# Modulation products on TensorE in four column groups of 32, with the first gate's row made per block

## The chip, the cores and the metric

The kernel runs on one core of a Trainium2 chip. Its time is device microseconds (us) of one execution of the program; before the change the median of 3 runs is 2649.36 us (2646.62 to 2649.52). The engines are TensorE (PE: matmuls; PEld is its weight load, which overlaps them), VectorE (DVE), ScalarE (ACT), GpSimd (POOL) and SyncE (SP), which here issues every DMA, in program order.

## The reference, cut to what matters

Two transformer-like blocks over x of 256 tokens by 2048 features, in fp32. The change lies in the first block, whose norms and gates are modulated by a vector c:

```python
c_act = jax.nn.silu(c)                       # 1 x 2048
mod = c_act @ w_ada[l] + b_ada[l]            # w_ada: 2048 x 12288 (96 MB)
sh1, sc1, gt1, sh2, sc2, gt2 = jnp.split(mod, N_MOD, axis=-1)
h = modulate(rmsnorm(x, g_norm_mix[l]), sh1, sc1)
proj = h @ w_in[l]                           # 2048 x 3072
...                                          # convolution, RG-LRU, gelu gate, pooling mixer
y = jnp.concatenate([y_lru, y_pool], axis=-1) @ w_out[l]
x = x + gt1[:, None, :] * y
h = modulate(rmsnorm(x, g_norm_ffn[l]), sh2, sc2)
f = (jax.nn.silu(h @ w_ffn_gate[l]) * (h @ w_ffn_up[l])) @ w_ffn_down[l]
x = x + gt2[:, None, :] * f
```

So a matrix of 96 MB is multiplied by one row. sh1 and sc1 are needed before w_in, gt1 after w_out's first block of columns, the rest for the feed-forward part.

## The kernel before, in words

The big matrices are streamed once, in tiles of 1 MB, through four slots (`raw`). ACT rounds each half tile to `w_hi` (`split_hi`, L634), DVE takes the rest into `w_lo` (`split_lo`, L1803), and PE forms three products per chunk (hi·hi, lo·hi, hi·lo). A matrix is a `Phase`: blocks of 512 columns, each of 8 halves; a half is 24 matmuls of 256 columns in w_in (`features_half`, L1175 to L1177) and 12 of 512 columns in the others (`tokens`, L1200 to L1202). `stream`, `mixer` and `beside` functions hang other work between the halves; the order is written out by hand, there is no scheduler.

The modulation matrix comes in tiles of 128 x 1024 (512 KB). A unit `a` is 1024 of its output columns, 16 tiles deep; there are 12 units, 192 tiles.

- **First stage** (units 0 to 3 in the order `MOD_ORDER`, 64 tiles, eight slots: `mod_raw` and `mod_more`): nothing else can start before shift and scale are known. 26 of the tiles go to PE (`first_product`, L1305): the stationary operand is a column of `c_silu` spread over 128 columns, so all 128 rows of the result are equal. The other 38 go to DVE (L2043, L2047), which multiplies a tile by a scalar per partition and adds it to `mod_acc`. DVE adds PE's row to it (`add_rows`, L2060), and PE sums `mod_acc` over the partitions with `ones` as the moving operand (`first_sums`, L1313). Between the products stand x's transposes (`TURN0_AT`) and w_in's first halves (`W_IN_AT`); the fourth half follows the last sums.
- **Later** (units 4 to 11, 128 tiles, the four `mod_raw` slots): all on DVE, beside the halves (`mod_product`, L2017 and L2021). `mod_places` says how many tiles each half carries: 48 beside w_in's 48 halves, 48 beside w_out's 32, 32 in the feed-forward part. PE sums a unit when it is done (`mod_sums`, L1293), DVE adds the bias (`mod_result`).
- **The first gate**: after w_in PE spreads all 16 chunks of gt1 over the partitions (`rows_of`, L1273), ACT copies them to `row` (L884) before it splits w_out's next halves, and DVE uses `row` after each block of w_out (`add_gated`, L2230, L2232).

SP issues a modulation tile once the tile four (first stage: eight) before it has been used, and a weight tile once DVE has taken `w_lo` of the one in its slot (L516). The queue is in order: a tile whose slot isn't free holds back whatever is behind it.

Of the kernel before, what the change touches and what calls it, by code (L numbers as in the profile page):

```python
# [26 lines left out]
P = 128  # L27
# [5 lines left out]
LEAD = 3  # L33
# [53 lines left out]
def two_blocks(nc, d, out):  # L87
# [58 lines left out]
    mod_places = [2, 1, 1, 1, 2, 1, 1, 1] * 3 + [1, 1, 1, 0, 1, 1, 1, 0] * 3 + [2] * 20 + [1] * 8 + [0] * 4 + [1, 0] * (4 * up1.halves)  # L146
    assert MOD_FIRST * KC + sum(mod_places) == MOD_BLOCKS * KC and MOD_FIRST == 4 and MOD_BLOCKS == 12

    MOD_ORDER = [0, 2, 1, 3]
    FIRST_SLOTS = 2 * MOD_SLOTS  # L150
    mod_on_pe = [k in ((1, 3, 5, 7, 9, 11, 13, 15), (1, 4, 7, 10, 13))[i // 2] for i in range(MOD_FIRST) for k in range(KC)]
    FIRST_BY_DVE = mod_on_pe.count(False) + MOD_FIRST
    ROWS_AFTER = 14

    def mods_used(s):

        own = mod_on_pe[:s + 1].count(mod_on_pe[s])
        return own if mod_on_pe[s] else own + (s // KC + (s % KC > ROWS_AFTER))

    def mods_of_pe(i, k=KC):  # L160
        return mod_on_pe[i * KC:i * KC + k].count(True)

    def steps_of_dve(i):

        return mod_on_pe[:i * KC].count(False) + i

    def mod_at(place):

        n = MOD_FIRST * KC + sum(mod_places[:place])
        return range(n, n + mod_places[place])  # L170

    with ExitStack() as ctx:
# [21 lines left out]
        row = at("row", R, [P, D])  # L194
# [24 lines left out]
        gt2 = at("gt2", F + 90, [P, COLS])  # L219
# [25 lines left out]
        res_tmp = at("res_tmp", F + 88, [P, T, COLS])  # L245
# [60 lines left out]
        def first_rows(i):  # L306
            return (pair[:, 0], pair[:, 1], misc[:, 2:4], pair[:, 1])[i]
# [27 lines left out]
        def columns(tile, widths):  # L335
# [4 lines left out]
        ssq, var, std, rstd, c_silu, g_mod, ls8, nls8, window_inv, ssq_parts, scale, squared = columns(  # L340
            keep, [T, T, T, T, KC, KC, RC, RC, 16, T * 4, T, T])
# [33 lines left out]
        row_mm, row_ready, gt2_row, fin_x = (sem(n) for n in ("row_mm", "row_ready", "gt2_row", "fin_x"))  # L375
# [38 lines left out]
        GT2_AT = 1  # L414
# [34 lines left out]
        def _(pool):  # L449
# [5 lines left out]
            pool.memset(vec_rows[:], 0.0).then_inc(zeroed, 1)  # L455
            done(pool.memset(upper[:], 1.0))
# [5 lines left out]
                               pattern=[[1, P]], channel_multiplier=-1).then_inc(consts, 1)  # L462

# [17 lines left out]
        CONSTS = 6 + HALF_ROPE  # L481
# [3 lines left out]
        def _(sp):  # L485
            ada = d["w_ada"][0].rearrange("(k p) n -> p k n", p=P)

            def slot_free(s):

                sp.wait_ge(mod_used if mod_on_pe[s] else mod_step, mods_used(s))  # L490

            def load_first(s):
                if s >= FIRST_SLOTS:
                    slot_free(s - FIRST_SLOTS)
                sp.dma_start(first_slot(s), ada[:, s % KC, bass.ds(MOD_ORDER[s // KC] * MOD_COLS, MOD_COLS)]).then_inc(mod_landed[s % FIRST_SLOTS], 16)

            def load_mod(a, k):
                j = (a - MOD_FIRST) * KC + k
                if j < MOD_SLOTS:
                    slot_free(MOD_FIRST * KC - FIRST_SLOTS + j)  # L500
                else:

                    sp.wait_ge(mod_step, FIRST_BY_DVE + j + 1 - MOD_SLOTS)
                sp.dma_start(mod_raw[:, k % MOD_SLOTS, :], ada[:, k, bass.ds(a * MOD_COLS, MOD_COLS)]).then_inc(mod_landed[k % MOD_SLOTS], 16)
# [27 lines left out]
            def load_mods(place):  # L532
                if 0 <= place < len(mod_places):
                    for n in mod_at(place):
                        load_mod(n // KC, n % KC)
# [85 lines left out]
        def _(act):  # L621
# [100 lines left out]
            def norm_beside(n, gain=None):  # L722

                def finish(b, c):
                    if b:
                        norm_sums(n, b - 1)
                        norm_turned(n, b - 1, gain)
                return finish

# [61 lines left out]
            for t in range(T):  # L791
                run(xn_sq[:, t, :], x[:, t, :], ACT.Square, accum_out=ssq[:, t:t + 1]).then_inc(n_ssq, 1)
            act.wait_ge(vec_turned, 1)
# [12 lines left out]
            run(sin_t, ang_r, ACT.Sin).then_inc(prep_exp, 1)  # L806
            for b in range(XB):
                norm_turned(0, b)
            for q in range(XG):
                norm_high(0, q)  # L810
                if q < XG // 2:
                    split_hi(w_in, 0, [q])
                if q == XG // 2 - 1:
                    split_hi(w_in, 0, [4])
# [4 lines left out]
            def mixer(b):  # L819

                for n in range(w_in.halves):
# [4 lines left out]
                    beside(b, n)  # L826
                act.wait_ge(w_used, w_in.end(b))
# [55 lines left out]
            act.wait_ge(row_mm, 1)  # L883
            run(row[:], flat(misc[:]), ACT.Copy).then_inc(row_ready, 1)  # L884


            stream(w_out, norm_beside(1), up1)
# [14 lines left out]
            def beside_down1(b, place):  # L902
# [4 lines left out]
                if place == (GT2_AT if b else LAST_HIDDEN + 1):  # L907
                    act.wait_ge(gt2_row, b + 1)
                    if b:
                        act.wait_ge(res_ready, w_out.blocks + b)  # L910
                    run(gt2[:], misc[:, 2, :], ACT.Copy).then_inc(row_ready, 1)
# [249 lines left out]
        def _(pe):  # L1161
# [98 lines left out]

            def gt2_rows(b):

                pe.wait_ge(mod_ready, 10)
                if b:
                    pe.wait_ge(row_ready, b + 1)
                for m in range(4):
                    mm = pe.transpose(misc[:, 2, m * P:(m + 1) * P], mod[:, 5 * KC + 4 * b + m:5 * KC + 4 * b + m + 1].to_broadcast([P, P]), ident[:])
                mm.then_inc(gt2_row, 1)

            def rows_of(col, signal):  # L1270

                for m in range(KC):
                    mm = pe.transpose(misc[:, m // 4, (m % 4) * P:(m % 4 + 1) * P], col[:, m:m + 1].to_broadcast([P, P]), ident[:])  # L1273
                mm.then_inc(signal, 1)

# [11 lines left out]
            def mod_sums(a, c, read=None):  # L1287
                pe.wait_ge(mod_step, FIRST_BY_DVE + (a - MOD_FIRST) * KC + KC)
                if read:

                    pe.wait_ge(mod_ready, read)
                for m in range(MOD_M):
                    mm = pe.matmul(misc[:, 3, bass.ds(a * MOD_M + m, 1)], mod_acc[:, c, m * P:(m + 1) * P], ones[:, 0:1],  # L1293
                                   start=True, stop=True, skip_group_check=True)
                mm.then_inc(mod_mm, 1)

            def first_product(i, k):
# [3 lines left out]
                if i == 3 and not mods_of_pe(i, k):  # L1301

                    pe.wait_ge(mod_ready, 2)
                for e in range(2):
                    mm = pe.matmul(first_rows(i)[:, e, :], c_silu[:, k:k + 1].to_broadcast([P, P]), first_slot(s)[:, e * COLS:(e + 1) * COLS],  # L1305
                                   start=(mods_of_pe(i, k) == 0), stop=(mods_of_pe(i, k) + 1 == mods_of_pe(i)))
                mm.then_inc(mod_used, 1)

            def first_sums(i):

                pe.wait_ge(mod_step, steps_of_dve(i + 1))
                for m in range(MOD_M):
                    mm = pe.matmul(first_rows(i)[:, 0, m:m + 1], mod_acc[:, i % 2, m * P:(m + 1) * P], ones[:, 0:1],  # L1313
# [1423 lines left out]
```

## Time and profile before

| what | value |
|---|---|
| median of 3 runs | 2649.36 us |
| profiled execution, and its span | 2653.23 us, 2651.5 us |
| PE, DVE, ACT busy | 97%, 63%, 47% of the span |
| DMA | 549.44 MB, 207 GB/s over the span |
| mean granted TensorE clock | 0.987 |

The profile divides the program into a long part that PE fills and a beginning that it doesn't:

```profile
PE   6799989999999999999999999999999999999998
DVE  4788897674544455565777676546666666644444
ACT  2236335444444444444566655445555555544453
DMA  9997897886555555565534544555555555555554
```

Each digit is a fortieth of the span (66 us), in tenths busy. The first six are what the change is about: the first stage, w_in and w_out, with DMA at 0.9 and DVE high. From the seventh on, PE is full. Busy time of PE adds up matmuls that overlap in its pipeline, so idle time understates what is free there, and matmul counts over a stretch say more.

### The profile page before, as it was taken

The page shows a single profiled execution, that of the slowest core. Times are in us where ns is not written, and L with a number is a line of the kernel's source. Part 1 is how long each engine was busy: PE and PEld are TensorE (multiplying, and loading weights), DVE is VectorE, ACT ScalarE, POOL GpSimd, SP SyncE. Part 2 cuts the span into 40 slices and gives each one's busy share as a digit, 9 for nine tenths or more (in the row PEclk, how much of TensorE's full clock was granted, in tenths as well). Part 3 has the DMA queues.
Part 4 walks back from the last instruction along what each step waited for, and adds up shares of the span by engine and source line. Part 5 has one row for each costly group of instructions (what it writes and reads, how often), then busy time and mean ns, then how long its engine had stood idle before and what let it go on. Part 6 is the DMA issues. An engine that isn't in the chain of part 4 may idle for free.

```text
span 2651.5 us, 32416 instructions
## 1 busy us (share of the span) xinstructions
PE 2573.7 (97%) x12334; PEld 2127.8 (80%) x12334; DVE 1658.0 (63%) x1963; ACT 1257.5 (47%) x1637; POOL 5.6 (0%) x24
## 2 busy tenths in 40 slices
PE   6799989999999999999999999999999999999998
PEld 3589767888888888888888888888888888888877
DVE  4788897674544455565777676546666666644444
ACT  2236335444444444444566655445555555544453
POOL 0000000000000000000000000000000000000000
PEclk9899999999999999999999999999999999999999
DMA  9997897886555555565534544555555555555554
GB/s 346 359 365 262 317 365 240 283 270 198 188 187 188 189 186 187 186 206 175 164 123 128 159 127 137 185 192 186 190 186 180 188 181 183 186 186 186 187 194 143
DMA packets 350140, 549.44 MB, mean 207 GB/s; under 512 B 18496, under 2 KB 200784, under 8 KB 349264
## 3 DMA queue, kind: packets, MB, share of 16 engines
q1 hardware_dynamic: 350032, 547.94, 61.6%
q8 instruction: 75, 1.23, 0.2%
q14 instruction: 33, 0.27, 0.0%
HBM read 545.79 MB, written 2.10 MB: 207 GB/s over the span
## 4 chain that ended last, share of the span: by engine, by line
PE 84%; DVE 6%; DMA 6%; ACT 2%; issue 1%; SPq 1%; ACTq 0%; DVEq 0%
PE pair L1200 25%; PE pair L1202 25%; PE pair L1201 25%; DMA mod_raw<-in_w_ada 3%; DMA mod_more<-in_w_ada 2%; DVE mod_acc L2021 2%; DVE w_lo L1803 1%; PE pair L1730 1%; PE misc L1659 1%; PE misc L1783 1%; PE pair L1175 0%; ACT w_hi L634 0%; PE pair L1177 0%; PE pair L1176 0%; PE pair L1305 0%
## 5 line engine op out<-in xcount | busy, mean ns | idle before, releaser
L1803 DVE TENSOR_TENSOR w_lo<-raw,w_hi 128x1024 fp32r<-128x1024 f32 x848 | 1017.6, 1204 | 848.6 <-ACT w_hi L634 847.5
L634 ACT ACTIVATE w_hi<-raw 128x1024 fp32r<-128x1024 f32 x848 | 882.4, 1043 | 1091.5 <-PE pair L1202 1000.6
L1200 PE MATMUL pair<-w_hi,a_hi 128*128 128x512 f32 x2048 | 810.9, 396 | 6.7 <-DVE w_lo L1803 3.8
L1202 PE MATMUL pair<-w_hi,a_lo 128*128 128x512 f32 x2048 | 799.7, 390 | 0.0
L1201 PE MATMUL pair<-w_lo,a_hi 128*128 128x512 f32 x2048 | 798.7, 390 | 0.0
L1200 PEld LDWEIGHTS pair<-w_hi,a_hi 128*128 128x128 f32 x2048 | 385.5, 188 | 87.7 <-DVE w_lo L1803 5.0
L1202 PEld LDWEIGHTS pair<-w_hi,a_lo 128*128 128x128 f32 x2048 | 385.4, 188 | 81.7
L1201 PEld LDWEIGHTS pair<-w_lo,a_hi 128*128 128x128 f32 x2048 | 385.9, 188 | 78.0 <-issue 1.0
L1200 PE MATMUL pair<-w_hi,hid_hi 128*128 128x512 f32 x704 | 275.0, 391 | 0.0
L1202 PE MATMUL pair<-w_hi,hid_lo 128*128 128x512 f32 x704 | 274.0, 389 | 0.0
L1201 PE MATMUL pair<-w_lo,hid_hi 128*128 128x512 f32 x704 | 273.9, 389 | 0.0
L2021 DVE SCALAR_TENSOR_TENSOR mod_acc<-mod_raw,keep,mod_acc 128x1024 f32<-128x1024 f32 x120 | 153.8, 1282 | 16.8 <-DMA mod_raw<-in_w_ada 13.9
L1202 PEld LDWEIGHTS pair<-w_hi,hid_lo 128*128 128x128 f32 x704 | 132.2, 188 | 27.4
L1200 PEld LDWEIGHTS pair<-w_hi,hid_hi 128*128 128x128 f32 x704 | 132.2, 188 | 27.2
L1201 PEld LDWEIGHTS pair<-w_lo,hid_hi 128*128 128x128 f32 x704 | 132.2, 188 | 27.1
L1175 PE MATMUL pair<-a_hi,w_hi 128*128 128x256 f32 x384 | 115.1, 300 | 11.6 <-DVE w_lo L1803 11.6
L1176 PE MATMUL pair<-a_lo,w_hi 128*128 128x256 f32 x384 | 111.5, 290 | 0.0
L1177 PE MATMUL pair<-a_hi,w_lo 128*128 128x256 f32 x384 | 111.3, 290 | 0.0
L1175 PEld LDWEIGHTS pair<-a_hi,w_hi 128*128 128x128 f32 x384 | 76.9, 200 | 14.2 <-DVE w_lo L1803 13.1
L1176 PEld LDWEIGHTS pair<-a_lo,w_hi 128*128 128x128 f32 x384 | 76.8, 200 | 1.1 <-issue 1.0
L1177 PEld LDWEIGHTS pair<-a_hi,w_lo 128*128 128x128 f32 x384 | 76.6, 200 | 0.0
L1200 PE MATMUL pair<-w_hi,ya_hi 128*128 128x512 f32 x128 | 50.6, 395 | 0.9 <-DVE w_lo L1803 0.9
(369 smaller groups left out, 2148.7 us busy)
## 6 DMA issues: line engine op xcount, KB each, us to landing
raw<-in_w_in SPq DMA_DIRECT2D x88, 1024.0 KB, 5.4
raw<-in_w_up SPq DMA_DIRECT2D x176, 512.0 KB, 4.4
mod_raw<-in_w_ada SPq DMA_DIRECT2D x160, 512.0 KB, 6.8
raw<-in_w_out SPq DMA_DIRECT2D x48, 1024.0 KB, 5.1
raw<-in_w_ffn_gate SPq DMA_DIRECT2D x88, 512.0 KB, 3.6
raw<-in_w_ffn_up SPq DMA_DIRECT2D x88, 512.0 KB, 4.7
raw<-in_w_ffn_down SPq DMA_DIRECT2D x32, 1024.0 KB, 5.1
raw<-in_w_down SPq DMA_DIRECT2D x32, 1024.0 KB, 5.1
```

Source lines behind the costliest of these rows:

```text
L634: run(w_hi[:, h % HALF_SLOTS, 0:n, :], raw[:, h // 2 % RAW_SLOTS, at0:at0 + n, :], ACT.Copy).then_inc(hi_ready, 1)
L1175: pe.matmul(o, wh, hi[:, k, :], start=(h == kk == 0 and m % 2 == 0), stop=False, skip_group_check=True)
L1176: pe.matmul(o, wh, lo[:, k, :], start=False, stop=False, skip_group_check=True)
L1177: mm = pe.matmul(o, wl, hi[:, k, :], start=False, stop=(h == ph.halves - 1 and kk == n - 1), skip_group_check=True)
L1200: pe.matmul(o, hi[:, own], w_hi[:, slot, kk, :], start=(h == kk == 0), stop=False)
L1201: pe.matmul(o, hi[:, own], w_lo[:, slot, kk, :], start=False, stop=False)
L1202: mm = pe.matmul(o, lo[:, own], w_hi[:, slot, kk, :], start=False, stop=(h == ph.halves - 1 and kk == n - 1))
L1659: mm = pe.matmul(misc[:, h // 8, (h % 8) * SP:(h % 8 + 1) * SP], decay[:, h, :], xdt[:, c, h, :], start=True, stop=True, skip_group_check= ...
L1730: mm = pe.transpose(pair[:, c, m // 2, m % 2 * S + t * P:m % 2 * S + (t + 1) * P], ff_t[:, t, m * P:(m + 1) * P], ident[:])
L1783: mm = pe.matmul(misc[:, j, :], p_f[:, k, t * P:(t + 1) * P], w_ple[:, k, j * COLS:(j + 1) * COLS], start=(k == 0), stop=(k == PLE // P - 1))
L1803: dve.tensor_tensor(w_lo[:, slot, 0:n, :], raw[:, h // 2 % RAW_SLOTS, at0:at0 + n, :], w_hi[:, slot, 0:n, :].bitcast(F32), ALU.subtract).t ...
L2021: dve.scalar_tensor_tensor(out=acc, in0=of, scalar=by, in1=acc, op0=ALU.mult, op1=ALU.add).then_inc(mod_step, 1)
```

## The change

All 64 tiles of the first stage, and 32 of the later 128 (units 5 and 6), are multiplied on PE. The stationary operand is now a column of `c_silu` spread over 32 columns, and each product writes 32 partitions of one bank: an even tile's two halves of columns write partitions 0 to 31 and 32 to 63, an odd tile's the other two quarters. ACT copies the bank to `mod_rows` (`mod_out`), and four small matmuls with `mod_rows` stationary and `groups` (a 128 x 2 matrix of ones at partitions 0 and 64, and 32 and 96) moving add the quarters and turn the row into columns (`mod_turn`). Sixteen tiles that stood beside w_out now stand beside w_in. gt1's row is made for one block of 512 columns at a time.

```diff
-    mod_places = [2, 1, 1, 1, 2, 1, 1, 1] * 3 + [1, 1, 1, 0, 1, 1, 1, 0] * 3 + [2] * 20 + [1] * 8 + [0] * 4 + [1, 0] * (4 * up1.halves)
+    mod_places = [2, 1, 1] * (IN_PLACES // 3) + [2, 1, 1, 1, 1, 1, 1] * 4 + [0] * 4 + [1, 0] * (4 * up1.halves)
+    MOD_BY_PE, MOD_BY_DVE = [5, 6], [4, 7, 8, 9, 10, 11]
+        order = "PPD" * 8 + "D" * 8 + "DDPP" * 8 + "D" * 32 + "D" * 32
...
+            def mod_product(k, tile, bank):
+                for e in range(2):
+                    own = slice((2 * (k % 2) + e) * (P // 4), (2 * (k % 2) + e + 1) * (P // 4))
+                    mm = pe.matmul(bank[own], c_silu[:, k:k + 1].to_broadcast([P, P // 4]), tile[:, e * COLS:(e + 1) * COLS],
+                                   start=(k < 2), stop=(k >= KC - 2), skip_group_check=True)
+                mm.then_inc(mod_used, 1)
...
+            def mod_turn(a, count):
+                pe.wait_ge(mod_turned, count)
...
+                for m in range(MOD_M // 2):
+                    mm = pe.matmul(mod_cols(a)[:, m:MOD_M:MOD_M // 2], mod_rows[:, m * P:(m + 1) * P], groups,
+                                   start=True, stop=True, skip_group_check=True)
...
+            def mod_pair(n):
+                for j in (n - 1, n):
+                    pe.wait_ge(mod_landed[j % MOD_SLOTS], 16 * (FIRST_TILES // FIRST_SLOTS + j // MOD_SLOTS + 1))
...
+                for j in (n - 1, n):
+                    mod_product(mod_seq[j][1], mod_raw[:, j % MOD_SLOTS, :], misc[:, 3, :])
...
             for i in range(MOD_FIRST):
                 for k in range(KC):
-                    if mod_on_pe[i * KC + k]:
-                        first_product(i, k)
+                    first_product(i, k)
+                    if i and k == 1:
+                        mod_turn(MOD_ORDER[i - 1], i)
...
-                first_sums(i)
+            mod_turn(MOD_ORDER[MOD_FIRST - 1], MOD_FIRST)
             first_w_in(3)
...
+                def beside_w_in(h):
+                    if b == 0 and h == 4:
+                        pe.wait_ge(mod_ready, MOD_FIRST)
+                        mods_beside(0)
+                    mods_beside(b * w_in.halves + h - LEAD)
...
-            rows_of(mod[:, 2 * KC:3 * KC], row_mm)
...
-                    dve.tensor_tensor(res_tmp[:], pair[:, c], row[:, None, cols].to_broadcast([P, T, COLS]), ALU.mult).then_inc(res_ready, 1)
+                dve.tensor_tensor(pair[:, c], pair[:, c], gt[:, None, :].to_broadcast([P, T, COLS]), ALU.mult).then_inc(res_ready, 1)
```

Where a unit's sums and results fall is set by `SUMS_AT` and `RESULT_AT`. On DVE the first stage keeps the norm of x and loses its 38 products.

PE's queue at the program's start, before (`pair` is the PSUM result, `keep` holds `c_silu`, `mod_more_79` and `_80` are the further slots):

```order
L1305 MATMUL pair<-mod_raw,keep 128x512 x4
L1305 MATMUL pair<-mod_more_79,keep 128x512 x2
L1305 MATMUL pair<-mod_more_80,keep 128x512 x2
L1305 MATMUL pair<-mod_raw,keep 128x512 x4
L1305 MATMUL pair<-mod_more_79,keep 128x512 x2
L1284 MATMUL misc<-ident,vec_rows 128x128 x7
L1305 MATMUL pair<-mod_more_80,keep 128x512 x2
L1313 MATMUL pair<-ones,mod_acc 128x1 x8
```

and now (two rows per tile, so x8 is four tiles):

```order
L1347 MATMUL pair<-mod_raw,keep 32x512 x8
L1347 MATMUL pair<-mod_more_78,keep 32x512 x4
L1347 MATMUL pair<-mod_more_79,keep 32x512 x4
L1347 MATMUL pair<-mod_raw,keep 32x512 x8
L1347 MATMUL pair<-mod_more_78,keep 32x512 x4
L1320 MATMUL misc<-ident,vec_rows 128x128 x7
L1347 MATMUL pair<-mod_more_79,keep 32x512 x4
L1347 MATMUL pair<-mod_raw,keep 32x512 x4
L1339 MATMUL misc<-keep,mod_rows 128x2 x4
```

PE has twice the products per unit, a quarter as wide, and the sums of a unit stand behind the first two tiles of the next.

DVE's queue where w_in's first block is under way, before (`w_lo` is the half's split, `mod_acc` a modulation tile, `a_lo` the normalised x):

```order
L1899 TENSOR_TENSOR a_lo<-features_70,a_hi 128x512 x2
L2017 TENSOR_SCALAR mod_acc<-mod_raw,keep 128x1024
L2021 SCALAR_TENSOR_TENSOR mod_acc<-mod_raw,keep,mod_acc 128x1024 x3
L1803 TENSOR_TENSOR w_lo<-raw,w_hi 128x1024
L2021 SCALAR_TENSOR_TENSOR mod_acc<-mod_raw,keep,mod_acc 128x1024
L1803 TENSOR_TENSOR w_lo<-raw,w_hi 128x1024
L2021 SCALAR_TENSOR_TENSOR mod_acc<-mod_raw,keep,mod_acc 128x1024 x2
L1803 TENSOR_TENSOR w_lo<-raw,w_hi 128x1024
```

and now:

```order
L1983 TENSOR_TENSOR a_lo<-features_69,a_hi 128x512 x2
L2102 TENSOR_SCALAR mod_acc<-mod_raw,keep 128x1024
L1886 TENSOR_TENSOR w_lo<-raw,w_hi 128x1024
L2106 SCALAR_TENSOR_TENSOR mod_acc<-mod_raw,keep,mod_acc 128x1024
L1886 TENSOR_TENSOR w_lo<-raw,w_hi 128x1024 x3
L2106 SCALAR_TENSOR_TENSOR mod_acc<-mod_raw,keep,mod_acc 128x1024
L1886 TENSOR_TENSOR w_lo<-raw,w_hi 128x1024 x2
```

Two of three modulation tiles there are gone from DVE. They stand in PE's queue, two tiles (four products) at a time between w_in's halves:

```order
L1214 MATMUL pair<-a_hi,w_hi 128x256
L1215 MATMUL pair<-a_lo,w_hi 128x256
L1216 MATMUL pair<-a_hi,w_lo 128x256
L1347 MATMUL misc<-mod_raw,keep 32x512 x4
L1214 MATMUL pair<-a_hi,w_hi 128x256
L1215 MATMUL pair<-a_lo,w_hi 128x256
L1216 MATMUL pair<-a_hi,w_lo 128x256
```

Of the 16 such pairs, 15 stand in w_in and one behind w_out's third half. Of the first eight, six stand two halves behind the one before, one three halves; from the ninth on they are three apart.

## Rows read from the trace of the kernel before

**Rows 1.** Stretches: busy us of PE, PEld, DVE, ACT, POOL; PEclk, DMA share, GB/s.

```profile
0.00:60.00 60.00, 41.05 (x102) 18.92 (x103) 26.27 (x52) 16.76 (x20) 5.56 (x24) 0.91 0.91 339
60.00:116.00 56.00, 42.37 (x181) 26.64 (x180) 41.24 (x46) 9.52 (x12) 0.00 (x0) 0.87 1.03 404
116.00:187.00 71.00, 61.89 (x458) 61.28 (x459) 61.86 (x76) 27.09 (x33) 0.00 (x0) 0.88 0.93 337
187.00:285.00 98.00, 95.08 (x734) 92.22 (x734) 88.16 (x92) 56.82 (x77) 0.00 (x0) 1.00 0.81 290
285.00:404.00 119.00, 105.17 (x474) 84.38 (x473) 106.74 (x92) 43.47 (x50) 0.00 (x0) 0.96 0.93 339
430.00:700.00 270.00, 270.00 (x1232) 224.14 (x1231) 167.62 (x150) 114.55 (x121) 0.00 (x0) 1.00 0.75 250
```

**Rows 2.** The same view, shorter stretches of the first stage and one of w_in.

```profile
25.00:35.00 10.00, 5.45 (x17) 2.10 (x15) 2.37 (x3) 0.18 (x1) 0.16 (x1) 1.00 0.82 293
45.00:50.00 5.00, 5.00 (x10) 2.02 (x10) 2.57 (x2) 4.97 (x5) 0.00 (x0) 0.76 0.79 270
...
60.00:100.00 40.00, 32.14 (x132) 18.67 (x130) 32.05 (x38) 8.47 (x11) 0.00 (x0) 0.87 1.03 407
...
202.00:222.00 20.00, 20.00 (x168) 19.97 (x167) 14.05 (x13) 17.60 (x28) 0.00 (x0) 1.00 0.74 262
```

**Rows 3.** Order of time, PE: one tile's products; start, us, instruction.

```profile
97.51 1.88 PE L1305 MATMUL pair<-mod_more,keep 128*128 128x512 f32 x4
```

**Rows 4.** The chain that ended last, from 105 us: start, us, what.

```profile
96.80 11.46 DMA mod_more<-in_w_ada
...
108.29 1.29 DVE mod_acc L2047
...
109.68 1.22 DVE mod_acc L2060
...
110.99 1.30 DVE mod_acc L2047
...
112.33 3.59 PE pair L1313 x16
```

**Rows 5.** Groups of instructions, DVE, 116 to 285 us: busy, mean ns, idle before.

```profile
L2021 DVE SCALAR_TENSOR_TENSOR mod_acc<-mod_raw,keep,mod_acc 128x1024 f32<-128x1024 f32 x45 | 57.7, 1282 | 8.0 <-DMA mod_raw<-in_w_ada 7.2
L1803 DVE TENSOR_TENSOR w_lo<-raw,w_hi 128x1024 fp32r<-128x1024 f32 x46 | 56.2, 1223 | 10.7 <-ACT w_hi L634 10.7
```

**Rows 6.** Order of time, ACT: results of w_in's blocks 0, 2, 3, 5 leave PSUM.

```profile
138.75 1.93 ACT L784 ACTIVATE xc<-pair,vec 128x256 f32<-128x256 f32 x4 [2.04 <-PE pair L1177]
...
193.01 1.02 ACT L871 ACTIVATE xp<-pair 128x1024 f32<-128x1024 f32 x1 [1.98 <-PE pair L1177]
...
225.35 1.02 ACT L877 ACTIVATE xp<-pair 128x1024 f32<-128x1024 f32 x1 [1.76 <-PE pair L1177]
...
283.56 1.02 ACT L881 ACTIVATE y_lru<-pair 128x1024 f32<-128x1024 f32 x1 [2.03 <-PE pair L1177]
```

**Rows 7.** DMA issues, 122 to 290 us: count, KB each, median us to landing.

```profile
mod_raw<-in_w_ada SPq DMA_DIRECT2D x48, 512.0 KB, 6.8
raw<-in_w_in SPq DMA_DIRECT2D x18, 1024.0 KB, 7.4
```

**Rows 8.** Order of time, DVE: the longest wait for a tile in w_in.

```profile
155.76 1.28 DVE L2021 SCALAR_TENSOR_TENSOR mod_acc<-mod_raw,keep,mod_acc 128x1024 f32<-128x1024 f32 x1 [5.89 <-DMA mod_raw<-in_w_ada]
```

**Rows 9.** Groups of instructions, 122 to 290 us: small work on PE, the row copy.

```profile
L1293 PE MATMUL misc<-ones,mod_acc 128*128 128x1 f32 x32 | 3.7, 245 | 0.0
...
L1273 PE MATMUL misc<-ident,mod 128*128 128x128 f32 x16 | 2.0, 276 | 0.0
...
L884 ACT ACTIVATE row<-misc 128x2048 f32<-128x2048 f32 x1 | 1.9, 1867 | 0.0
```

**Rows 10.** Groups of instructions, 290 to 410 us: DVE's modulation products beside w_out.

```profile
L2021 DVE SCALAR_TENSOR_TENSOR mod_acc<-mod_raw,keep,mod_acc 128x1024 f32<-128x1024 f32 x45 | 57.7, 1283 | 8.0 <-DMA mod_raw<-in_w_ada 5.8
```

**Rows 11.** Chain of waits, 385 us: x's eight transposes beside a block of w_out.

```profile
385.88 1.09 PE misc L1230 x8
```

## What I expect of the change

> **What bounds the kernel now.** I read the busy time by stretches first, then the order of time at the seams, the groups of instructions, and last the landing times of the DMAs.
>
> [rows 1] cut the first 430 us at the seams of the stages. To 116 us only x's transposes, three halves of w_in and modulation products run, and DMA is the limit: 404 GB/s at a share of 1.03 from 60 us on. In the first 60 us it is 339 GB/s, with holes where slots were freed late, 293 from 25 to 35 us and 270 from 45 to 50 [rows 2]. w_in (116 to 285 us) has no single limit. In its first 71 us PE is busy 61.9 at a clock of 0.88, DVE 61.9 and DMA 0.93. In the next 98 us PE is busy 95.1 at full clock. In w_out (285 to 404) DVE is busy 106.7 of 119 us and DMA 0.93, and PE waits for both. From 430 us on PE is full and the change touches nothing that it waits for.
>
> What PE needs at full clock: 168 matmuls of 256 columns in 20 us [rows 2], 0.119 us each, so a half of w_in (24) is 2.88 us; 1232 of 512 columns in 270 us [rows 1], 0.219 each, so a half of w_out (12) is 2.63 us and its 32 halves 84 us.
>
> **The price of a product.** This is what the whole sum hangs on. One tile on PE is four records in 1.88 us [rows 3], though the code asks for two products: an fp32 product passes through the array twice. The last record's tail is some 0.59 us, so a pass is (1.88 - 0.59) / 3 = 0.43 us, a product 0.86, a tile 1.72. No row of before shows a product on 32 columns. Bounds: if nothing overlaps, a pass takes what it took, since its 512 columns still stream by: 1.72 us a tile. If all four quarters stream together, two tiles take two passes, 0.86 us. I take the middle. The two passes of one product use the same 32 columns and must follow each other, and they stand next to each other in the queue. The second pass can then overlap only with the first pass of the next product. That makes 0.43 us per product, 0.86 per tile in a row of tiles, and for two tiles alone between w_in's halves five steps of 0.43, 2.15 us, with some 0.28 for the pipeline at both ends: 2.43 us.
>
> The Trainium skill (TensorEngine Tiling (Array Packing), Key Properties) says that tiles of the array operate independently and that a change of tiling mode drains the engine; the overlap and the 0.28 agree with that in kind, and nothing in this trace shows it. It also says (TensorE: Matmul & The Clock Gate, Measured speedup vs the span model) that three column tiles ran 2.38 times as fast as one after the other. By that figure, as an estimate, two tiles would take 3.44 / 2.38 = 1.45 us and not 2.43, and the sum below would be 16 us lower.
>
> **Part by part, in the profiled execution.**
>
> 1. First stage. PE now takes all 64 tiles: 64 x 0.86 = 55 us, up to 64 x 1.29 = 83 when each tile comes alone. Beside it, 3 halves of w_in 8.6, four times the transposes at 1.09 [rows 11] 4.4, vectors and turns some 4: 72 to 100 us in the 100 that DMA needs. DMA stays the limit. Slots are now freed by one engine that is quicker per tile (0.86 against 1.28 on DVE [rows 5]) and never waits for `add_rows` or sums. The 15 us of holes in [rows 2] cost 10 x (407 - 293) / 407 + 5 x (407 - 270) / 407 = 4.5 us; the small loads' wait stays, so I count 3. At the end the chain was: tile landed 108.3, DVE product, PE's row added, DVE product, sixteen half-clock sums until 115.9 [rows 4], 7.6 us. Now: two products and tail 1.3 us, the ACT copy of 128 x 512 some 0.6, four small products (eight passes at 0.12) 1.0, with gaps 3.2 us. That is 4.4 less, and since PE isn't idle for 5 us before the sums, the clock's fall to half behind it (the sixteen sums' 3.59 us, [rows 4], and the half after them) mostly goes: 2 us. Sum: -9.4 us.
>
> 2. w_in, first 18 halves with pairs (116 to 187). Eight pairs, 8 x 2.43 = +19.4 us. Against it: 458 matmuls were done in 71 us [rows 1] where 458 x 0.119 = 54.5 are needed; 16.5 us are idle time or half clock. DVE keeps 8 of its 23 products there and is rid of 15 x 1.28 = 19 us [rows 5], so its share of this goes. The wait for DMA (5.89 us in one piece, [rows 8]) stays, now on PE. I let the pairs fill 8.7 of the 16.5. +10.7 us.
>
> 3. w_in, the rest (187 to 285), where PE was full. Seven pairs, +17.0. One of the two sums (3.7 / 2 = 1.85 us, [rows 9]) becomes a turn of 1.0: -0.9. The 16 transposes of the row go (-2.0) and ACT's copy of it, which held w_out's first halves (-1.9) [rows 9]. PE's idle 2.9 us [rows 1] shrinks by 2.0. +10.2 us.
>
> 4. w_out. PE: 84 + three transposes 3.3 + four gate rows at half of 1.09, 2.2 + the last pair 2.4 + one turn 1.0 + three sums 5.6 = 98.5 us. DVE drops from 106.7 by 16 x 1.28 [rows 10] to 86. DMA: 8.4 of its 119 x 0.339 = 40 MB move away, the remaining 32 MB take 80 us at 404 GB/s. PE becomes the limit; with 4 us for seams 102.5 against 119: -16.5 us. The row per block is made three halves before it is used; its cover is w_out's own halves, and if ACT were late for one, a block would start up to 1 us late.
>
> Sum: -9.4 + 10.7 + 10.2 - 16.5 = -5.0 us on 2653.2, that is 2648.2. The profiled execution was 3.9 us above the median of the runs, so 2644.3; I say 2644. Own range 2636 to 2653, from what parts 1, 2 and 4 may be off by (3, 6 and 4 us).
>
> **Rivals.**
>
> A. No overlap. A pair costs 3.44 + 0.3, 16 x 1.31 = 21 us more, and the first stage turns from DMA to PE: 64 x 1.72 + 17 = 127 us from 6 us on, 133 against 106, +27. 2644 + 48 = 2692. The same first stage would come if 32 columns left the clock at its lower level (0.87 is granted there now, [rows 1]); for it speaks that the clock already falls there with PE 42 of 56 us busy, against it that a slower PE would be busy without gaps. The doubled pass in [rows 3] speaks neither way.
>
> B. All four quarters at once. A pair costs 0.86 + 0.3, 16 x 1.27 = 20 us less on PE. But w_in then has to move 24 weight tiles (25 MB) and 64 modulation tiles (34 MB) in some 160 us, 370 GB/s, and its first 71 us had DMA at 0.93 with 337 [rows 1]; I let 12 of the 20 through: 2632. Against it stands the order of the passes.
>
> C. PE waits for tiles: the one that ends slower. DVE could be late by 5.9 us [rows 8] while PE had other halves to do. A pair in PE's queue that waits holds every half behind it, then `w_hi` and `w_lo` of the next, and through their slots SP. Six of the first eight pairs need a tile that is issued when the pair before has ended, two halves or 5.8 us earlier; the median landing is 6.8 us [rows 7]. That is 1 us short, and with SP held up by the tile ahead for some 1.5 us, six times 2.5 is +15: 2659. It decides from landings of about 6.5 us. Against it: with PE slower, the stretch asks for 3.67 MB (1.5 weight and 4 modulation tiles) in 3 halves and 1.33 pairs, 11.9 us, 309 GB/s, where it was 337 [rows 1], so the queue ahead of a tile is shorter than when 6.8 was measured.
>
> **How the numbers follow.** Forecast 0.50, A 0.15, B 0.16, C 0.15; 0.04 is left for the lower clock alone, slower. 0.2% is 5.3 us, about what a measurement here can tell from no change, so faster begins below 2644.1. The forecast gives 0.26 faster, 0.22 same, 0.02 slower; B 0.16 faster; C 0.04 same and 0.11 slower; A and the clock 0.19 slower. Faster 0.42, same 0.26, slower 0.32. The range leaves out most of A: from 2628 (B and its spread) to 2668 (C and its spread).
>
> **What would show it.** Eight 32-column records of a pair in five steps of 0.43 us mean the forecast, in eight steps A, in two B. The first record of w_in's fourth half should start at about 108 us; before it followed the sums of [rows 4] at 116. w_in's block 2 should leave PSUM within 3 us of 193.0, block 5 some 11 us later than 283.6 [rows 6], and w_out should end near 399, not 404. C shows as PE idle before the 32-column products with a DMA as releaser, over 10 us in w_in. If the first stage ends after 125 us, or w_out still takes over 110, the forecast is wrong.

## The result

The changed kernel takes 2657.18 us (median of 9 runs, 2654.90 to 2662.22), the kernel before 2649.52 beside it (9 runs, 2646.44 to 2656.48). The ratio is 1.0028, 95% interval 1.0016 to 1.0040: about 7 us slower. The prediction said 2644 and gave slower 0.32. The time lies in its range (2628 to 2668), the direction is wrong.

### The profile page after: what moved, and what is told of

It is laid out like the page before. It is cut to its first block, busy times and chain, and to the rows that moved or that the text cites. A ratio compares the mean times of both kernels' runs of the same rounds, so it can differ in the third digit from the quotient of the medians.

```text
span 2655.3 us, 32780 instructions
## 1 busy us (share of the span) xinstructions
PE 2581.8 (97%) x12566; PEld 2107.5 (79%) x12566; DVE 1570.0 (59%) x1891; ACT 1260.9 (47%) x1646; POOL 5.9 (0%) x27
## 4 chain that ended last, share of the span: by engine, by line
PE 88%; DMA 4%; DVE 4%; ACT 2%; SPq 1%; issue 1%; ACTq 0%; DVEq 0%
PE pair L1239 26%; PE pair L1241 26%; PE pair L1240 26%; DMA mod_raw<-in_w_ada 3%; DMA mod_more<-in_w_ada 1%; DVE w_lo L1886 1%; PE pair L1214 1%; PE pair L1215 1%; PE pair L1216 1%; PE pair L1813 1%; PE pair L1347 1%; PE misc L1742 1%; PE misc L1866 1%; PE misc L1269 1%; DVE mod_acc L2106 0%
## 5 line engine op out<-in xcount | busy, mean ns | idle before, releaser
L2106 DVE SCALAR_TENSOR_TENSOR mod_acc<-mod_raw,keep,mod_acc 128x1024 f32<-128x1024 f32 x90 | 115.3, 1281 | 66.4 <-DMA mod_raw<-in_w_ada 64.8
```

What stands on the lines that cost most here:

```text
L2106: dve.scalar_tensor_tensor(out=acc, in0=of, scalar=by, in1=acc, op0=ALU.mult, op1=ALU.add).then_inc(mod_step, 1)
```

## The profile after

The profiled executions took 2655.3 and 2651.5 us of span. The same stretches as [rows 1], busy us of PE, PEld, DVE, ACT and POOL, then the granted clock as a share, DMA share and GB/s; the last two lines are of the first stage and answer to [rows 2]:

```profile
0.00:60.00 60.00, 35.20 (x144) 9.03 (x144) 5.67 (x35) 16.45 (x20) 5.90 (x27) 0.80 0.86 317
60.00:116.00 56.00, 47.58 (x266) 20.21 (x263) 12.25 (x24) 12.00 (x15) 0.00 (x0) 0.93 1.03 406
116.00:187.00 71.00, 63.99 (x486) 54.86 (x485) 38.21 (x52) 25.83 (x31) 0.00 (x0) 0.94 0.93 324
187.00:285.00 98.00, 91.03 (x678) 82.91 (x677) 79.95 (x80) 51.58 (x70) 0.00 (x0) 0.98 0.83 312
285.00:404.00 119.00, 113.25 (x584) 93.24 (x583) 95.08 (x89) 48.19 (x57) 0.00 (x0) 0.99 0.89 325
45.00:50.00 5.00, 3.49 (x16) 2.18 (x20) 3.07 (x20) 1.45 (x4) 0.00 (x0) 0.50 0.47 190
50.00:55.00 5.00, 5.00 (x34) 1.55 (x27) 0.00 (x0) 0.00 (x0) 0.00 (x0) 0.66 0.76 224
```

DVE has over a third less to do from 116 to 187 us (38.2 against 61.9), and the stage is no faster. The first 60 us move less than before (317 GB/s against 339). Four marks cut the difference: the first matmul of w_in's fourth half, block 5 leaving PSUM, the first matmul of w_out, and the last squares of its result. In the order of time of the kernel before:

```profile
115.77 0.56 PE L1175 MATMUL pair<-a_hi,w_hi 128*128 128x256 f32 x1
...
285.15 0.48 PE L1200 MATMUL pair<-w_hi,pool_hi 128*128 128x512 f32 x1
...
404.10 0.61 ACT L697 ACTIVATE squares_a<-x_res 128x512 f32<-128x512 f32 x1
```

and after, where 200.34 and 300.12 answer to 193.01 and 283.56 in [rows 6]:

```profile
114.73 0.49 PE L1214 MATMUL pair<-a_hi,w_hi 128*128 128x256 f32 x1
...
200.34 1.02 ACT L898 ACTIVATE xp<-pair 128x1024 f32<-128x1024 f32 x1 [2.53 <-PE pair L1216]
...
300.12 1.02 ACT L908 ACTIVATE y_lru<-pair 128x1024 f32<-128x1024 f32 x1 [2.03 <-PE pair L1216]
...
305.74 0.63 PE L1239 MATMUL pair<-w_hi,pool_hi 128*128 128x512 f32 x1 [4.67 <-DVE pool_lo L2256]
...
410.23 0.61 ACT L710 ACTIVATE squares_a<-x_res 128x512 f32<-128x512 f32 x1
```

| stage | before | after | difference | forecast |
|---|---|---|---|---|
| first stage, to w_in's fourth half | 115.8 | 114.7 | -1.0 | -9.4 |
| w_in, to block 5 out of PSUM | 167.8 | 185.4 | +17.6 | +24.8 |
| seam, to w_out's first matmul | 1.6 | 5.6 | +4.0 | -3.9 |
| w_out | 119.0 | 104.5 | -14.5 | -16.5 |
| sum | | | +6.1 | -5.0 |

(The forecast's -2.0 and -1.9 for the transposes and the copy of the gate's row belong to the seam here. The 6.1 us are still there when down1's matmuls start, at 913.6 against 907.4 us. The two profiled spans differ by only 3.8 us, so the rest went in the part that the change doesn't touch. Each kernel has one trace; the first mark falls within 0.8 us in the seven kernels that are the same up to there (113.95 to 114.73), and that is the measure for small differences between traces.) Three things stand out.

**A pair is cheap.** Order of time, PE, a pair and the matmul behind it:

```profile
122.14 1.06 PE L1347 MATMUL misc<-mod_raw,keep 128*32 128x512 f32 x8
123.13 0.39 PE L1214 MATMUL pair<-a_hi,w_hi 128*128 128x256 f32 x1
```

Eight records in 1.06 us, and w_in goes on 0.99 us after the pair's start. The forecast had 2.43, rival B 1.16.

**In the first stage one wait on PE stops the transfers.** Order of time, PE, ACT and SP:

```profile
39.28 1.25 PE L1347 MATMUL pair<-mod_raw,keep 128*32 128x512 f32 x4
46.51 1.86 PE L1339 MATMUL misc<-keep,mod_rows 128*128 128x2 f32 x8 [5.98 <-ACT mod_rows L804]
```

```profile
38.81 3.89 ACT L820 ACTIVATE xn<-x_res,keep 128x2048 f32<-128x2048 f32 x2 [0.23 <-DVE keep L2142]
...
45.88 0.58 ACT L804 ACTIVATE mod_rows<-pair 128x512 f32<-128x512 f32 x1
```

```profile
39.93 11.14 SPq L504 DMA_DIRECT2D mod_raw<-in_w_ada  x4
```

The first unit's sums are complete before 39.28 us, but ACT's copy of them (`mod_rows`) stands in its queue behind x's scaling (`xn`), two table loads and four small activations. `mod_turn` waits for it in PE's queue, right behind the second tile of the next unit. The products behind it free no slots, SP takes 11.14 us for four tiles, and the transfers fall to 190 and 224 GB/s.

**In w_in DVE and SP wait.** The waits, 116 to 300 us for DVE and to 302 for PE and SP: waiter, releaser, us in total, times, longest. After:

```profile
DVE mod_acc L2106 <- DMA mod_raw<-in_w_ada: 50.0, 12, 8.0
```

```profile
PE pair L1214 <- DVE w_lo L1886: 8.2, 9, 2.3
PE misc L1347 <- DMA mod_raw<-in_w_ada: 4.8, 1, 4.8
```

```profile
SPq L517 <- PE misc L1347: 118.9, 14, 13.7
SPq L517 <- DVE mod_acc L2106: 20.2, 16, 3.3
```

and of SP before:

```profile
SPq L516 <- DVE w_lo L1803: 75.9, 20, 8.6
SPq L504 <- DVE mod_acc L2021: 49.5, 31, 6.5
SPq L504 <- DVE mod_acc L2017: 25.7, 3, 15.6
```

For 119 of 186 us SP, which issues every transfer in order, stands before a slot that PE frees. SP did not wait less before: up to 285 us, where w_in ended, 134.7 of 169 us, but for DVE alone. What is new is that DVE's own tiles stand behind a slot of PE. One instance, in the order of time of SP, PE and DVE, and the same stretch by windows:

```profile
227.40 0.33 SPq L517 DMA_DIRECT2D mod_raw<-in_w_ada  x1
227.77 0.43 SPq L529 DMA_DIRECT2D raw<-in_w_in  x1
228.25 1.69 SPq L517 DMA_DIRECT2D mod_raw<-in_w_ada  x3
229.99 0.46 SPq L529 DMA_DIRECT2D raw<-in_w_in  x1
```

```profile
226.30 1.06 PE L1347 MATMUL misc<-mod_raw,keep 128*32 128x512 f32 x8
```

```profile
236.53 2.67 DVE L2106 SCALAR_TENSOR_TENSOR mod_acc<-mod_raw,keep,mod_acc 128x1024 f32<-128x1024 f32 x2 [5.54 <-DMA mod_raw<-in_w_ada]
```

```profile
222.00:227.00 5.00, 5.00 (x45) 4.33 (x43) 3.34 (x4) 4.92 (x6) 0.00 (x0) 1.00 0.00 0
```

From 222 to 227 us nothing is transferred. PE's pair ends at 227.36, SP issues 0.04 us later, and the two tiles that DVE wants next are in that burst. DVE has nothing else to do from 230.99 and waits until 236.53. By the code that is built in. With four slots and the order D D P P (D a tile for DVE, P one for PE), a tile of DVE is issued behind a tile of PE, whose slot comes free after PE's half q; DVE, which runs three halves ahead, reaches its product when it has split half q + 4, and that split, too, waits for PE's half q (four split slots). So DVE wants the tile when it is only being asked for.

This one wait costs PE nothing: from 230 to 245 us PE is busy 14.86 of 15 us at full clock. Of DVE's 50 us of waits only a part reaches PE: at most 8.2 us before w_in's matmuls, in nine pieces, and 4.67 us in the seam. The other 4.8 us are PE's own wait for a tile.

## The experiments

Ratios are to the kernel before, run beside each, with a 95% interval. Its median there was 2651.2 to 2652.0 us and not 2649.52, so a difference of times to the changed kernel may be off by 2 to 3 us; by the ratios such a gain is larger by up to that. A "place" is the stretch beside one half of w_in or w_out. Two theories at the start. **T**: PE's own time for the pairs is what lengthened w_in. **W**: DVE's waits for tiles behind PE's slots did. "Block 5" is the time at which it leaves PSUM (300.12 in the changed kernel).

**1. pairs_small**

```diff
-                    mod_product(mod_seq[j][1], mod_raw[:, j % MOD_SLOTS, :], misc[:, 3, :])
+                    mod_product(mod_seq[j][1], mod_raw[:, j % MOD_SLOTS, :], misc[:, 3, :], 16 if 2 <= mod_seq[j][1] < 14 else COLS)
```

> Twelve of the sixteen pairs of 32-column products that TensorE does beside w_in run over 16 columns of each half tile instead of 512 (that part of the modulation is left out); tiles, waits, signals and order stay. Theory T (TensorE's own time: a pair costs it 1.2 us and nothing hides it): twelve pairs lose about 1.0 us each, w_in's last block leaves PSUM about 12 us earlier than 300.1 us, the kernel is 10 to 13 us faster than the changed one, near 2645. Theory W (VectorE, stopped for tiles whose slots TensorE frees, is what lengthened w_in; TensorE's products fall into its idle time): VectorE's 50 us of waits stay, w_in is at most 3 us shorter, the kernel 2654 to 2658.

2655.89 us, ratio 1.0012 (1.0003 to 1.0022). Block 5 at 295.70: 4.4 us of the 9.6 taken from PE (twelve times 1.06 less 0.26). DVE still waits 46.1 us, and PE's waits for DVE rise from 8.2 to 13.3. The time is in W's range, the 4.4 us are over its 3; T's 12 is far off.

**2. pairs_twice**

```diff
+                    if 2 <= k < 14:
+                        mod_product(mod_seq[j][1], mod_raw[:, j % MOD_SLOTS, :], misc[:, 3, :], signal=False)
```

> The same twelve pairs of products are done twice on TensorE (this part of the modulation is counted twice), before the signal that frees the tiles. Theory T: twelve times 1.1 to 1.2 us, w_in 13 to 15 us longer, the kernel near 2671. Theory W: the products fall into TensorE's idle time and the tiles are freed at most 1.2 us later, w_in at most 4 us longer, the kernel 2657 to 2662. The forecast's price (2.43 us for a pair) would make it 29 us longer, near 2686.

2659.83 us, ratio 1.0033 (1.0020 to 1.0045). A doubled pair is 16 records in 1.92 us, so PE got 12 x 0.86 = 10 us more, and block 5 came out at 299.64, no later at all (w_in itself 0.3 us longer). PE's idle time before w_in's matmuls fell from 8.2 to 3.8 us in place of it. The profiled execution was 2.3 us under the median; even so the kernel pays at most 3 us for the 10. T is out for the kernel as changed.

**3. one_group**

```diff
+                    if one_group:
+                        own = slice(0, P // 4)
```

> The same twelve pairs send all four quarters' products to the first column group, one after the other (their sums land in the wrong rows of that unit). If the products of a pair run side by side only because they stand in different column groups, eight records of 0.43 us stand in a row: a pair takes 3.4 us instead of 1.06, twelve pairs 28 us, the kernel near 2685 by theory T (their time is on the path) and near 2665 by theory W. If the groups have nothing to do with it, a pair stays at 1.06 us and the time at 2657.

2666.95 us, ratio 1.0060 (1.0044 to 1.0077). Order of time, PE, a pair:

```profile
128.19 3.62 PE L1349 MATMUL misc<-mod_raw,keep 128*32 128x512 f32 x8
```

3.62 us against 1.06 for the same eight passes: the column groups make the overlap, a factor of 3.4 for four groups. The Trainium skill (TensorEngine Tiling (Array Packing), Key Properties) says that the tiles work independently; the trace agrees, and shows that the two passes of an fp32 product do not stand in the way. Of the 12 x 2.56 = 31 us more on PE, w_in took 10.7 (block 5 at 310.81): the slack in w_in is about 20 us. Not all of it is idle time: from w_in's fourth half to block 5 PE's idle time falls from 14.0 to 3.8 us, and the granted clock rises from 0.96 to 1.00.

**4. dve_three_later**

```diff
-                for n in mod_at(place):
+                for n in mod_at(place - 3) if place >= 3 else ():
                     if mod_seq[n][0] in MOD_BY_DVE:
                         mod_product(n)
```

> VectorE does its modulation products of a place three places later, at the time at which TensorE does its own, so that the tiles behind a slot that TensorE frees have some 15 us more to land. Theory W: VectorE's 50 us of waits for tiles between 116 and 300 us fall under 10, w_in's last block leaves PSUM 8 to 15 us earlier than 300.1, the kernel 2642 to 2650. Theory T: the waits fall just the same, but TensorE had only 8 us of idle time behind VectorE and 5 behind tiles there, of which a part goes: 2652 to 2656.

2643.18 us, ratio 0.9969 (0.9957 to 0.9982): 14 us faster than the changed kernel. The waits, 116 to 300 us:

```profile
DVE mod_acc L2106 <- DMA mod_raw<-in_w_ada: 1.7, 2, 1.0
```

50 us of waits became 1.7, and block 5 comes at 292.07. w_in is 7.7 us shorter, the seam 4.7 (0.9 us in place of 5.6), w_out 1.6. W holds against T. But the edit moves DVE's products behind three more splits, too, so it doesn't tell the landing from the order on DVE; 11 and 12 come back to that.

**5. turn_later**

```diff
-                    if i and k == 1:
+                    if i and k == (8 if i == 1 else 1):
                         mod_turn(MOD_ORDER[i - 1], i)
```

> TensorE takes the first unit's turn (mod_turn) seven tiles later, after tile (1, 8) instead of (1, 1), so it no longer stands before the products of the tiles at 40 to 46 us while ScalarE has not yet copied the unit's rows (it did so at 45.88 us). Theory (the hole in the transfers at 40 to 55 us cost the first stage its gain): 45 to 50 and 50 to 55 us move over 270 and 320 GB/s as before the change, the last tile of the first stage lands near 108.5 instead of 112.1 us, w_in's fourth half starts 3 to 4 us earlier than 114.87, the kernel 3 to 4 us below the changed one. Rival (the transfers are held by something else in these 15 us, the vectors' small loads, or the tail waits for other steps): at most 1 us.

2651.82 us, ratio 1.0002 (0.9993 to 1.0011), 5 us less than the changed kernel. Windows, and the first matmul of w_in's fourth half:

```profile
45.00:50.00 5.00, 3.68 (x18) 1.02 (x18) 2.60 (x17) 1.09 (x4) 0.00 (x0) 1.00 1.02 410
50.00:55.00 5.00, 4.70 (x31) 1.82 (x32) 0.17 (x1) 1.02 (x1) 0.00 (x0) 1.00 1.02 405
```

```profile
109.28 0.36 PE L1214 MATMUL pair<-a_hi,w_hi 128*128 128x256 f32 x1
```

The hole is gone and not only back at what it was before the change, and the gain is more than expected: 5.4 us earlier than 114.73, where 3 to 4 were expected. The other hole of [rows 2], 25 to 35 us, stays (299 GB/s, 293 before the change).

**6. both_mended** (4 and 5 together)

> The later turn and VectorE's products three places later together. If the two causes are independent: 2643.2 less 3 to 4, 2639 to 2641, some 9 to 11 us faster than before the change. Rival (w_in's start is set by VectorE's and ScalarE's splits, or TensorE's tiles come no earlier): as with the three places alone, 2642 to 2644.

2637.56 us, ratio 0.9952 (0.9938 to 0.9966). w_in's fourth half starts at 109.54 and block 5 leaves at 285.13. The two causes add up.

**7. all_by_dve_old_places**

```diff
-    MOD_BY_PE, MOD_BY_DVE = [5, 6], [4, 7, 8, 9, 10, 11]
+    MOD_BY_PE, MOD_BY_DVE = [], [4, 5, 6, 7, 8, 9, 10, 11]
```

with `mod_places` of before and the sums' places to match.

> The later tiles as before the change: all 96 by VectorE, at the places of before (48 beside w_in, 48 beside w_out); the first stage on TensorE and the gate's row per block stay. Theory: these two parts are worth what the profile after shows, 0.8 us in the first stage and some 2 us (the sixteen transposes and the row's copy between w_in and w_out), so 2646 to 2649 against 2650 to 2652 of before. Rival (the gate's row per block delays w_out's blocks, or the first stage leaves w_in's start worse): 2652 to 2657.

2650.85 us, ratio 0.9998 (0.9989 to 1.0007). The first stage and the row per block are worth nothing that can be told from zero: between theory and rival.

**8. all_by_dve_new_places** (the same, with the change's `mod_places`)

> The places of the change (64 tiles beside w_in, 32 beside w_out), but all tiles by VectorE. Theory: VectorE has 64 times 1.28 us of products and 53 us of splits there and 16 tiles more than before, 20.5 us of work for some 17 us of idle time in 169; w_in 8 to 15 us longer than before, w_out 12 to 16 us shorter, the kernel 2642 to 2650, at most as fast as with the three places. If TensorE's share and not the late tiles had been the trouble, it would be faster than dve_three_later, under 2640. Rival (the share of w_in's transfers, not VectorE, sets it): w_in no more than 4 us longer, 2635 to 2640.

2644.39 us, ratio 0.9975 (0.9965 to 0.9985). DVE is full as expected, and PE waits for it (116 to 300 us):

```profile
PE pair L1214 <- DVE w_lo L1886: 20.4, 7, 6.5
```

Block 5 comes at 291.79, 7.8 us later than in 7, and w_out's last squares at 396.18 instead of 404.94 us. So moving sixteen tiles from w_out to w_in is worth some 6 us with all of them on DVE. Giving 32 of them to PE as the change does costs 13 (2657.18 against 2644.39); with DVE's products three places later it costs nothing that can be told (2643.18).

**9 and 10. mended_pairs_small, mended_pairs_twice** (the edits of 1 and 2 in both_mended)

> In both_mended, the twelve pairs over 16 columns instead of 512 (that part of the modulation is left out), as in pairs_small. There the same edit brought only 4.4 us in w_in of the 9.6 that it takes from TensorE (twelve times 1.06 less 0.26). Theory: since VectorE no longer stands behind tiles, TensorE sets w_in's pace and its products lie on the path: w_in 7 to 10 us shorter, the kernel 2628 to 2631. Rival (something else, the transfers or the splits, still sets it, and the pairs are hidden): at most 4 us, 2634 to 2637.

> In both_mended, the twelve pairs done twice (counted twice in that part of the modulation), as in pairs_twice, where this added some 10 us to TensorE and 2.7 to the kernel. Theory: here it is all on the path, 9 to 11 us, 2646 to 2649. Rival (hidden as there): 2638 to 2641.

2631.10 us, 0.9925 (0.9909 to 0.9942), and 2641.92 us, 0.9967 (0.9957 to 0.9977). Neither theory is met in size. 9.6 us less on PE made w_in 3.3 us shorter (block 5 at 282.52 from 285.13, after a start 0.7 us later) and the kernel 6.5 us faster; 10 more made w_in 4.5 us longer (289.67) and the kernel 4.4 us slower. PE's waits for tiles went the other way, 12.9 and 4.8 us against 8.8. So once DVE is free of waits, the pairs do cost time, about half of what they take on PE, and the transfers hold the rest; that last part is argued from PE's waits.

**11 and 12. dve_one_later, dve_two_later** (with the later turn)

> The later turn, and VectorE's products one place later instead of three. The tiles that come late were asked for when TensorE freed a slot, and VectorE wanted them then: each place later gives them one half of TensorE, 2.9 to 3.9 us. Theory: the 12 waits of together 50.3 us of turn_later fall to 8 to 20 us, and more than half of the 14 us between turn_later (2651.8) and both_mended (2637.6) is there: 2641 to 2646. Rival (the order of the two on VectorE matters, not the landing): one place does as much as three, or nothing at all.

> The same, two places later. Theory: waits for tiles under 5 us, 2638 to 2641, within 2 us of three places. Rival as for one place.

2637.81 us, 0.9948 (0.9931 to 0.9965), and 2632.66 us, 0.9933 (0.9916 to 0.9949). Waits of DVE for tiles, 116 to 300 us, with the turn alone, one, and two places later:

```profile
DVE mod_acc L2106 <- DMA mod_raw<-in_w_ada: 50.3, 12, 7.5
```

```profile
DVE mod_acc L2106 <- DMA mod_raw<-in_w_ada: 33.7, 12, 6.1
```

```profile
DVE mod_acc L2106 <- DMA mod_raw<-in_w_ada: 18.4, 9, 5.9
```

The waits shrink by some 16 us for each place, 1.4 for each of twelve, where I had expected 2.9 to 3.9, and both times lie under the expected ranges (2641 to 2646, 2638 to 2641). One place brings 14 us with 33.7 us of waits left, as much as three places do: this is what the rival said, that the order of product and split on DVE matters and not the landing. The second place, with 15 us less of waits, brings 5 more, which the rival doesn't give. So the sum of DVE's waits is not what the kernel pays. That only the part of a wait counts that outlasts PE's queued halves would fit both; this is argued, not shown, and the share of landing and order stays open.

What PE loses is on record. From w_in's fourth half to block 5, before, after, and with two places:

```profile
115.77:283.56 167.79, 155.76 (x1178) 152.29 (x1179) 148.73 (x165) 82.88 (x109) 0.00 (x0) 0.95 0.86 309
114.73:300.12 185.39, 171.41 (x1286) 152.77 (x1289) 125.43 (x140) 83.21 (x110) 0.00 (x0) 0.96 0.86 311
109.30:280.48 171.18, 165.04 (x1286) 148.21 (x1289) 129.72 (x146) 83.05 (x110) 0.00 (x0) 0.99 0.93 336
```

PE is idle 12.0, 14.0 and 6.1 us, at a granted clock of 0.95, 0.96 and 0.99. The changed kernel's w_in is 14.2 us longer than that of two places for the same work: 7.8 us more idle time, and 6.4 us more busy time at the lower clock. With one place PE is idle 10.1 us at 0.98, with three 9.5 at 0.98.

Two places are best, 0.67% or some 18 us under the kernel before. SP's waits, for DVE's and PE's slots, in both_mended and then in dve_two_later, suggest why three are worse:

```profile
SPq L517 <- DVE mod_acc L2106: 73.4, 27, 10.0
SPq L517 <- PE misc L1347: 69.1, 14, 11.2
```

```profile
SPq L517 <- PE misc L1347: 96.9, 15, 11.1
SPq L517 <- DVE mod_acc L2106: 41.0, 20, 5.5
```

With three places DVE holds its own slots so long that SP waits 73 us for them, and PE waits 8.8 us for tiles instead of 5.4 (one piece of 5 us is in both, and in the changed kernel). That this is all of the 5 us between the two is argued, not shown.

The ends of dve_two_later's w_in and seam (w_in's fourth half starts at 109.30), ACT and PE:

```profile
280.48 1.02 ACT L908 ACTIVATE y_lru<-pair 128x1024 f32<-128x1024 f32 x1 [2.03 <-PE pair L1216]
```

```profile
282.61 0.50 PE L1239 MATMUL pair<-w_hi,pool_hi 128*128 128x512 f32 x1 [1.17 <-DVE pool_lo L2256]
```

w_in takes 171.2 us, 3.4 more than before with sixteen more tiles and fifteen pairs in it; the seam 2.1; the first stage is 6.5 shorter.

## Why the prediction was wrong

- **The price of a product failed.** "I take the middle", 2.43 us for a pair: it costs 1.0 (eight records in 1.06). All four quarters' passes stream together, which was rival B's assumption. The reason given against it, that the two passes of a product stand next to each other and must follow, was an argument from the code with no row behind it, and so was the 0.28 us for the pipeline's ends: w_in goes on 0.99 us after a pair's start, 0.13 more than two passes of 0.43. Alone, this error would have made w_in 15 x 1.4 = 21 us shorter than forecast; what follows ate that up. The Trainium skill's 2.38 for three column tiles (TensorE: Matmul & The Clock Gate, Measured speedup vs the span model), quoted there, gave the estimate of 1.45 us, nearer than my value; measured are 1.0 us, and a factor of 3.4 for four groups.
- **Part 1, first stage, failed:** -9.4 forecast, -1.0 measured. Slots were to be freed "by one engine that is quicker per tile ... and never waits for `add_rows` or sums". It waits for the turn, and the turn for a copy that stands late in ACT's queue. The tail's term was right in size (3.2 forecast; last product started 112.07, w_in went on at 114.73, 2.7), but the last tile landed 3.8 us later than before. The 2 us for the clock didn't come in full: PE was idle for 1.57 us at most before the turn, and the granted clock still fell to 0.50, from 116 to 118 us, as it was from 114 to 118 before. The later turn gives back 5.4 us; with it the stage is 6.5 us shorter than before, two thirds of the forecast.
- **Parts 2 and 3, w_in: two errors against each other.** +24.8 forecast, +17.6 measured. With the right price the same working gives 15 x 1.0 less the 11.6 that it let idle time and sums absorb, +3.4 us, and dve_two_later has just that (171.2 against 167.8). It does so by what the forecast counted on: PE's idle time falls by 5.9 us and the clock rises from 0.95 to 0.99. That the two agree to a tenth is luck. The rest came from what parts 2 and 3 took as gain: DVE "is rid of 15 x 1.28 = 19 us ..., so its share of this goes". Its busy time went, waits of 50 us took its place, and PE's idle time rose from 12.0 to 14.0 us where 8.7 of idle time or half clock were to be filled. Experiments 4 and 6 show the price of DVE's places: 8 and 10 us at block 5 (300.12 to 292.07; 295.38 to 285.13), 14 in the kernel both times, of which the seam has some 4.7. What of it is the tiles' landing and what the order on DVE is open (11).
- **The seam failed:** -3.9 forecast, +4.0 measured. The row's transposes did go, but a wait of DVE of 6.64 us, for a tile that landed at 298.78, held `pool_lo` and the split, and PE stood 4.67 us.
- **Part 4, w_out, held:** -16.5 forecast and 102.5 us long, -14.5 and 104.5 measured.
- **Rival C was the closest in sign and time (2659), for a mechanism one engine off.** It had "a pair in PE's queue that waits holds every half behind it ... and through their slots SP". PE waited 4.8 us once, and this wait is there with two places, too (5.0). It is DVE, in order and ahead of PE, that reached tiles whose slots PE had only just freed. C's test (PE idle over 10 us before 32-column products) would have cleared it wrongly. B had the right price of a pair and a wrong time, 2632, for the kernel as changed.

## What to carry over

When two engines at different distances from the data share a ring of slots and one in-order queue fills it, list for each tile which engine frees its slot and when the next reader wants it: the engine that runs ahead waits for the one behind plus a landing. Then look at what the far end of the chain loses, not at the sum of the waits: taking 50 us of waits from DVE brought 14. Moving DVE's products two halves later, nearer to PE's place in time, turned, together with the moved turn, a loss of 7 us into a gain of 18. And an instruction that waits for a slow helper must not stand in the queue of the engine that frees the slots.

## What I had not expected of the hardware

Two fp32 products on each of two tiles, sent to four column groups of 32, run as one: eight records in 1.06 us against 3.62 in one group, and a second set adds 0.86. Their weight loads take 0.11 us each against 0.19 for 128 columns. PE was idle for 5.98 us up to 46.51, and the granted clock was 0.50 (1.2 GHz) from 45 to 50 us; with the hole closed it was 1.00 (2.4 GHz) there.
